# Packed operand tiles that start 256 bytes, in place of 64 bytes, behind a multiple of 512 bytes

## What is computed

```python
def _conv_ffn(h, w_in, conv_w, conv_b, w_out):
    gate, up = jnp.split(h @ w_in, 2, axis=-1)
    return (jax.nn.silu(_dwconv(gate, conv_w, conv_b)) * up) @ w_out
...
def channel_mixer(h, w1, w2):
    return jnp.square(jax.nn.relu(h @ w1)) @ w2
...
        if l < DEPTH - 1:
            ctx_args = (None,) + mix_args[1:]
            h_ctx = h_ctx + mod_c[2] * token_mixers(zc, k1c, k2c, vc, *ctx_args)
```

## Time and profile before

| | |
|---|---|
| median of 3 runs | 2420.2 us (2415.12 to 2422.82) |
| the profiled execution | 2418.31 us, of which the span of instructions is 2416.2 us |
| TensorE busy | 2321.0 us, 96% of the span |
| VectorE, ScalarE, GpSimd busy | 70%, 42%, 1% |
| mean granted TensorE clock | 0.990 |
| read from HBM | 350.94 MB, 147 GB/s over the span with what is written |

### The profile page before, as it was taken

One profiled execution on the slowest core, in us unless ns is written; L12 is line 12 of the kernel. 1 busy time (PEld: TensorE's weight loads), 2 busy tenths in 40 slices (PEclk: granted clock), 3 DMA queues, 4 the chain that ended last, 5 costly groups with the idle time before them and its releaser, 6 DMA issues.

```text
span 2416.2 us, 31421 instructions
## 1 busy us (share of the span) xinstructions
PE 2321.0 (96%) x12350; PEld 1946.0 (81%) x12350; DVE 1683.9 (70%) x2754; ACT 1017.2 (42%) x1593; POOL 31.7 (1%) x65
## 2 busy tenths in 40 slices
PE   7999999999999999999899999999999999889998
PEld 4888878877787888887788999667788888768998
DVE  6876567455589886778768777787675454776655
ACT  4422322256624322224555545555432332465543
POOL 0000000010000000000000000000000000000000
PEclk9999999999999999999999999999999999999999
DMA  8355435542443444443314564212245344323554
GB/s 347 125 208 199 175 139 209 193 161 99 157 157 114 147 174 166 156 140 104 127 53 155 180 207 135 70 53 79 102 166 206 129 174 174 101 71 109 189 184 131
DMA packets 99132, 360.33 MB, mean 149 GB/s; under 512 B 11096, under 2 KB 14552, under 8 KB 96808
## 3 DMA queue, kind: packets, MB, share of 16 engines
q1 hardware_dynamic: 94600, 341.46, 40.5%
q0 software_dynamic: 4384, 16.86, 2.0%
HBM read 350.94 MB, written 5.24 MB: 147 GB/s over the span
## 4 chain that ended last, share of the span: by engine, by line
PE 80%; DVE 12%; ACT 5%; issue 2%; DMA 1%; SPq 0%; DVEq 0%; ACTq 0%
PE PS L673 62%; PE PS L873 3%; PE PS L701 3%; DVE w_lo L1954 3%; PE PS L1089 2%; ACT w_hi L1305 1%; PE PS L915 1%; PE PS L1280 1%; PE PS L889 1%; DVE conv L2767 1%; PE PS L733 1%; PE PS L1204 1%; ACT probs L1816 1%; DVE xv L2392 1%; DVE h_lo L2382 1%
## 5 line engine op out<-in xcount | busy, mean ns | idle before, releaser
L1954 DVE TENSOR_TENSOR w_lo<-raw,w_hi 128x1024 fp32r<-128x1024 f32 (+1 forms) x456 | 543.2, 1209 | 289.6 <-ACT w_hi L1305 288.0
L1305 ACT ACTIVATE w_hi<-raw 128x1024 fp32r<-128x1024 f32 (+1 forms) x456 | 460.5, 1041 | 461.1 <-PE PS L673 443.9
L673 PE MATMUL PS<-h_hi,w_hi 128*128 128x512 f32 (+1 forms) x1456 | 474.5, 334 | 5.0 <-DVE h_lo L2382 3.8
L673 PE MATMUL PS<-h_hi,w_lo 128*128 128x512 f32 (+1 forms) x1400 | 469.5, 335 | 0.0
L673 PE MATMUL PS<-h_lo,w_hi 128*128 128x512 f32 (+1 forms) x1336 | 450.9, 337 | 0.0
L673 PEld LDWEIGHTS PS<-h_hi,w_hi 128*128 128x128 f32 x1456 | 269.8, 188 | 34.0 <-issue 2.7
L673 PE MATMUL PS<-hid_hi,w_hi 128*128 128x512 f32 (+1 forms) x864 | 289.8, 335 | 2.5 <-DVE w_lo L1954 2.5
L673 PE MATMUL PS<-hid_hi,w_lo 128*128 128x512 f32 (+1 forms) x864 | 289.0, 334 | 0.0
L673 PE MATMUL PS<-hid_lo,w_hi 128*128 128x512 f32 (+1 forms) x864 | 288.6, 334 | 0.0
L673 PEld LDWEIGHTS PS<-h_hi,w_lo 128*128 128x128 f32 x1400 | 263.4, 188 | 27.6
L673 PEld LDWEIGHTS PS<-h_lo,w_hi 128*128 128x128 f32 x1336 | 251.7, 188 | 27.6 <-issue 0.2
(11 more groups left out here) (441 smaller groups left out, 3778.4 us busy)
## 6 DMA issues: line engine op xcount, KB each, us to landing
raw<-in_weights SPq DMA_DIRECT2D x434, 512.0 KB, 4.5
ada_ring<-in_ada SPq DMA_DIRECT2D x176, 512.0 KB, 3.7
raw<-in_weights SPq DMA_DIRECT2D x22, 384.0 KB, 4.0
og<-in_ada SPq DMA_DIRECT2D x4, 1024.0 KB, 11.7
qk<-in_ada SPq DMA_DIRECT2D x4, 1024.0 KB, 16.8
m_hi<-h_spill POOLq DMA_DIRECT2D x4, 1024.0 KB, 8.0
wgt<-in_x SPq DMA_DIRECT2D x4, 512.0 KB, 17.6
h_spill<-h_hi POOLq DMA_DIRECT2D x1, 2048.0 KB, 8.7
```

The lines of the kernel that those rows point to most:

```text
L673: mm = pe.matmul(out, a, b, start=(k == 0 and i == 0), stop=(k == ph.k_tiles - 1 and i == 2))
L1305: act.activation(w_hi[:, s, 0:w], raw[:, s, 0:w], ACT.Copy).then_inc(sem("w_hi"), 1)
L1954: dve.tensor_tensor(w_lo[:, s, 0:w], raw[:, s, 0:w], w_hi[:, s, 0:w].bitcast(F32), ALU.subtract)\
```

## The change

One constant. `OFF_LINE` goes from 16 to 64 elements, that is, from 64 to 256 bytes.

```diff
@@ -40,7 +40,7 @@
 BANKS = 4
 UNIT = 1024
 LINE = 512
-OFF_LINE = 16
+OFF_LINE = 64
 LEAD = 2
 CONV_TAPS = 11
 ADA_LAYER = 6 * D // P
```

## The result

The changed kernel takes 2421.44 us (median of 20 runs, 2419.33 to 2426.04) against 2417.75 us for the kernel before (20 runs, 2414.27 to 2422.82). The ratio is 1.0017, with a 95% interval of 1.0011 to 1.0023, so 3.7 us more by the medians, with an interval of 2.7 to 5.6. The time lies in the predicted range and within 0.3%, as forecast. The reason given for it does not hold: the spacing of the matmuls did change.

The account below looks back on a forecast made before the run. TensorE, with a matmul in it for 96% of the span, was taken as the bound. Terms 0 + 0.1 + 0 + 0 us on the 2420.2 us median gave 2420.3 us, whole range 2410 to 2429.

Parts of the forecast that it names:

- How many matmuls: Matmuls reading packed or folded tiles: 3600 move, so d ns in the spacing is worth 3.6 us times d.
- The price at 256 bytes: Packed-tile matmuls of 256 columns: 117.7 ns each at 256 bytes as at 64, so 3600 x 0 = 0 us.
- The repeat length of 256 bytes: Rival, 20%: 256 bytes acts like 0, all 3600 matmuls at 120.0 ns, +8.3 us, 2428.6 us.
- The unchanged sum in `aout`: Rounds in `aout` with starts 64, 128, 64 bytes take 353 ns, three times 117.7; so 128 costs what 64 does.
- From spacing to time: Packed phases `f1` and `g1`: each nanosecond between two matmul starts goes straight into the time.
- The rival "faster" at 115 ns: Rival, 15%: 256 bytes is better still, 115 ns throughout the packed matmuls, -9.7 us, 2410.6 us.
- Writers, copy, move of `out_low`: VectorE and ScalarE tile writers 0, hidden copy of `turn_hi` 0, low operands of `aout` moving onto the line +0.1 us.
- The page on TensorE: Trainium skill's N / 2.4 + 2.5 ns: 109.2 ns for 256 columns at any address; the prediction did not follow it.

Follow-up runs that it names:

- mixed_hi_lo: Kernel before with high and low parts at different starts: h high 64, low 0 bytes; hid high 0, low 64; one run, between 2414.52 and 2422.02 us.
- weights_64: Kernel before with only w_hi and w_lo moved, to 64 bytes behind a multiple of 512; 2456.23 us beside 2420.17 for one run of before.

## Why the prediction was right in the number and wrong in the reason

That 2421.44 us came so near to the forecast of 2420.3 is partly luck. Two errors worked against each other, a widening put at nothing and waits taken to give nothing back, and the three runs that it started from had a median 2.4 us above that of the 20.

*How many matmuls:* 3600, on which all followed; it held, since each packed phase changed and no unpacked one did.

*The price at 256 bytes:* this is the step that failed, as the prediction put it, "I take 117.7 ns for 256 bytes". It was 120.0. The two addresses off the line on which it leaned, 64 and 128, were taken for proof that off the line all is alike. The 128 in `aout` was one operand in three; with all three there the rhythm was 119.9 or 118.7. The repeat length of 256 bytes stood among the rivals, with 20%, and its fingerprint (63.0 us over 176 starts, loads of 192 ns) came out as written.

*The unchanged sum in `aout`* was read as "the operand costs what one at 64 does". `mixed_hi_lo` shows that prices of single operands do not add up, so that reading had no ground.

*From spacing to time:* "each nanosecond between two starts of matmuls goes straight into the time". True for the second block's half (3.6 of 3.8 us). In the first block's half about half of the 4.2 us falls into waits for VectorE. I had seen these waits and used them only to bound what the writers could cost. Had I chosen the right rival, I should have said +8.3 us, more than double the 3.7 measured.

*The rival "faster" at 115 ns* had a real cause behind it: rhythms under 117.7 exist (113.3 at distance 192 or, at times, 64; 116.7 at 32), but not at 256 bytes. The 115 itself was misread: 0.23 us for a pair in `aout` was taken for two distances of 115 ns, and the starts in the trace make a round there 118, 115 and 120.

*Writers, copy, move of `out_low`:* all at or near nothing, as said; `aout` after runs at 120.0 throughout and its 192 matmuls are among the 3600.

*The page on TensorE:* by the Trainium skill ("TensorE: Matmul & The Clock Gate", section "Back-to-back issue gap") the estimate was 109.2 ns at any address. The same section gives that formula for a matmul by itself and says that in a stream of weight loads and matmuls both set the spacing; the prediction left this out, and the formula was the wrong one for these streams. No rhythm of 256 columns in any of the fourteen kernels came below 113.2 ns, and they differ by up to 6.7 ns by address alone. By Part 2 of that page a weight load takes no read bandwidth from a running matmul. Whether it does here is not shown, but in `weights_64` moving only the weights changed the spacing of all products named above, so a matmul's pace was not independent of where its weights are read. The measurement decides.

What stays open is the mechanism under the rhythms. That it depends on the distance of the two operands modulo 256 bytes is shown, at the distances measured; that it is a conflict of the two read streams is only argued. What other engines read and wrote at the same time was not varied, and it may be what ends a rhythm where TensorE neither waited nor slowed its clock.

## What to carry to other kernels

Where TensorE is dense and each matmul has its own weight load, compare start-to-start distances between phases that should be alike; a steady difference of 2 ns over thousands of matmuls is worth a try with the operands' relative start, and what is good for one number of columns can be bad for another (distance 192 against 0 above). Before pricing a slower TensorE in full, look for its waits on another engine downstream: they take a part of it. Where the profile offers neighbours of an unmeasured value, ask whether they lie within one period of what may be a periodic effect.

## What the runs showed of the hardware that was not expected

- The distance modulo 256 bytes between stationary and moving tile, with the rhythm that a stream is in, sets the spacing of float32r matmuls with a weight load each: for 256 columns 120.0 ns at 0, 116.7 at 32, 117.7 or 113.4 at 64, 120.0 at 96, 118.7 or 119.9 at 128, 117.2 at 160, 113.3 or 117.7 at 192, 118.5 at 224. The dependence on the distance, and not on the moving tile's own start, was measured at 0 and 192.
- For 512 columns the order of these two is reversed: 226.9 ns at distance 0, 233.3 at 192. Moving the weights by 64 bytes cost 36 us in all.
- At distances 64, 128 and 192 two rhythms were seen, mostly steady over hundreds of matmuls. One changed behind a wait, one behind a stretch at the lower clock, and some with neither.
